# Two norms taken by token tile, the placing of crowded experts spread over four experts, and the last norm of block two read from its scatter banks

## The reference, cut to what matters

```python
def _rms(x, g):
    return x * rsqrt(mean(x * x, -1) + 1e-6) * g

x = x + mixed @ w_out                                         # stage "wo"
x = x + _mem_xattn(_rms(x, cross_norm_g), _rms(mem, ..), ..)  # norm "c", stages "mq", heads, "mo"
x = x + _hier_moe(_rms(x, ffn_norm_g), ..)                    # norm "r", routing, 32 experts
x = _rms(x, final_norm_g)
...
mod = silu(c) @ w_ada + b_ada                                 # stages "ada0" to "ada11"
...
# end of block two, alpha = 2 ** 0.25
ffn = hierarchical_moe(u2, ...)                               # 32 experts, 2 of them for a token
x = layernorm(alpha * x + g2 * ffn, ln2_g, ln2_b)
```

## Time and profile before

| what | value |
|---|---|
| median of three runs | 1096.92 us |
| the profiled execution, its time | 1097.21 us |
| its span | 1095.4 us |
| PE busy in the span | 979.4 us (89%) |
| DVE busy | 570.0 us (52%) |
| ACT busy | 362.1 us (33%) |
| POOL busy | 25.1 us (2%) |
| moved by DMA | 289.02 MB |

### The profile page before, as it was taken

How to read it: one execution, slowest core, us unless ns; L and a number is a source line. 1 busy time by engine, 2 the same in 40 slices (tenths; PEclk the granted TensorE clock), 3 DMA queues, 4 the chain that set the end, 5 groups by cost and what they waited for, 6 DMA issues and landing times. The chain is left out here.

```text
span 1095.4 us, 14594 instructions
## 1 busy us (share of the span) xinstructions
PE 979.4 (89%) x5138; PEld 588.3 (54%) x5138; DVE 570.0 (52%) x1067; ACT 362.1 (33%) x682; POOL 25.1 (2%) x49
## 2 busy tenths in 40 slices
PE   6999998988988799989999899988489998999962
PEld 5677558878665433433443588756444343344432
DVE  5844446554345444455444665866654445444436
ACT  5654244443332222211222457633332221122210
POOL 1000000000000000000000000000000000000001
PEclk9999999998995899999999999969589999999987
DMA  9264671444625599999999457311419999999800
GB/s 361 92 286 156 230 269 71 161 169 158 230 115 190 214 388 428 424 422 428 425 424 384 154 183 314 150 84 68 202 60 383 429 425 424 424 427 424 337 1 39
DMA packets 28607, 289.02 MB, mean 264 GB/s; under 512 B 3049, under 2 KB 5513, under 8 KB 7441
## 3 DMA queue, kind: packets, MB, share of 16 engines
q1 hardware_dynamic: 24768, 280.99, 62.9%
q0 software_dynamic: 1424, 4.79, 1.4%
q10 hardware_dynamic: 2368, 2.64, 0.7%
HBM read 287.34 MB, written 1.06 MB: 263 GB/s over the span
## 5 line engine op out<-in xcount | busy, mean ns | idle before, releaser
L942 PE MATMUL bank<-ring,arena 128*64 128x512 f32 x1040 | 242.5, 609 | 10.4 <-DVE arena L2114 6.6
L2128 DVE TENSOR_REDUCE arena<-bank 128x512 f32 x130 | 83.8, 686 | 142.1 <-PE bank L962 140.1
L477 DVE TENSOR_TENSOR ring_r<-ring,ring_r 128x1024 fp32r<-128x1024 f32 (+1 forms) x84 | 99.2, 1211 | 91.2 <-ACT ring_r L470 91.2
L942 PEld LDWEIGHTS bank<-ring,arena 128*64 128x64 f32 x1040 | 70.6, 139 | 136.9 <-issue 136.9
L956 PE MATMUL bank<-ring,arena 128*64 128x512 f32 x520 | 128.6, 616 | 8.3 <-DVE arena L2143 6.9
L606 PE MATMUL bank<-HT_r,ring_r 128*128 128x256 f32 x352 | 103.7, 295 | 10.3 <-DVE arena_r L1744 3.8
L470 ACT ACTIVATE ring_r<-ring 128x1024 fp32r<-128x1024 f32 (+1 forms) x84 | 84.9, 1047 | 83.4 <-PE bank L608 83.2
L608 PE MATMUL bank<-HT_r,ring_r 128*128 128x256 f32 x352 | 101.8, 289 | 0.0
L1499 ACT ACTIVATE arena<-bank 128x512 f32<-128x512 f32 x64 | 38.2, 597 | 167.9 <-PE bank L942 167.9
L1505 ACT ACTIVATE arena<-bank 128x512 f32<-128x512 f32 x64 | 38.2, 597 | 147.9 <-PE bank L956 147.9
L962 PEld LDWEIGHTS bank<-tab,arena 128*128 128x128 f32 x520 | 55.8, 140 | 53.7 <-issue 51.1
(11 more groups left out here) (403 smaller groups left out, 1350.4 us busy)
## 6 DMA issues: line engine op xcount, KB each, us to landing
ring<-in_experts SPq DMA_DIRECT2D x64, 2048.0 KB, 12.8
ring<-in_experts SPq DMA_DIRECT2D x64, 1024.0 KB, 9.2
ring<-in_ada SPq DMA_DIRECT2D x12, 2048.0 KB, 7.4
ring<-in_win SPq DMA_DIRECT2D x5, 2048.0 KB, 9.6
ring<-in_hy SPq DMA_DIRECT2D x3, 2048.0 KB, 18.8
ring<-in_mk SPq DMA_DIRECT2D x2, 2048.0 KB, 8.5
ring<-in_mv SPq DMA_DIRECT2D x2, 2048.0 KB, 10.0
ring<-in_wo SPq DMA_DIRECT2D x2, 2048.0 KB, 7.4
```

The lines of the kernel that those rows point to most:

```text
L477: nc.vector.tensor_tensor(R(w), w, R(h), ALU.subtract).then_inc(sem("w_low"), 1)
L942: last = mm(gu_bank[g:g + WIN, :], xw[:, k, :], w[:, k * 512:(k + 1) * 512], start=k < 2, stop=k >= KD - 2)
L2128: last = V.reduce_sum(ysT[:, 4 * u:4 * u + 4, bass.ds(s, WIN)], dT_bank[u][:, :].rearrange("p (c g w) -> p c w g", c=4, g=2), AXX)
```

## The change

1. `token_out` takes, in the last chunk alone, tile 0 with both `k` first and then tile 1.
2. Norms "c" and "r": ACT takes squares of half tiles (512 columns), the first halves between two `high` chunks, the second halves as soon as they are added; ACT computes the root of tile 0 and of tile 1 apart, and DVE inverts it (`deviations`, `scaled`). POOL has no part in it. For "c", DVE does `low(mq0, (0, 1))` before the last two additions and not behind them. ACT loads the table for roots before, and the table for exponentials behind.
3. `ada(6)` moves to between the `wo` product and the transposes, `ada(7)` to between the `mo` product and the transposes; their column sums go behind the transposes of "c" and behind the router product. `ada6` moves ahead of `mq0` in the ring, `ada7` behind `mo1`.
4. `extra_windows` is split into four parts that stand in experts 4 to 7 of the unrolled start of the loop, which DVE now has for eight experts and not for four.
5. DVE copies the columns of the first placed window before its last two `y_window`s, in both blocks, whether there is such a window or not. For this it waits for the table and reads `n` earlier; so does PE.
6. Block two: PE puts `alpha * X` into the scatter banks. DVE empties both down banks and multiplies with `g2row` while doing so; ACT's half is gone. DVE waits for `g2r` before the experts.
7. The end of block two: tile 0 gets its moments on DVE from the banks, tile 1 on ACT from the banks (copies with sums, then squares with sums). Each tile gets its own root on ACT, DVE scales in halves of 512 columns, and SP issues four stores of 256 KB.

```diff
-    + [(n, 4096) for n in ("mk0", "mk1", "mv0", "mv1", "wo0", "wo1", "mq0", "mq1", "ada6", "ada7", "mo0", "mo1",
+    + [(n, 4096) for n in ("mk0", "mk1", "mv0", "mv1", "wo0", "wo1", "ada6", "mq0", "mq1", "mo0", "mo1", "ada7",
                            "ada8", "ada9")]
...
+            for t in range(TT):
+                for u in range(2):
+                    sp.wait_ge(sem("x_end"), 2 * t + u + 1)
+                    sp.dma_start(out[t * P:(t + 1) * P, u * 512:(u + 1) * 512], X[:, t, u * 512:(u + 1) * 512]
+                                 ).then_inc(sem("stored"), 16)
...
-                        for a in range(2):
+                        last_chunk = c == CHUNKS - 1
+                        for t, a in sorted(itertools.product(range(TT), range(2)), key=lambda ta: ta if last_chunk else ta[::-1]):
                             k = 2 * c + a
-                            for t in range(TT):
...
+            ada(6)
             transposed("cT", XN, KD, "xn_c")
+            ada_col(6)
             channel_out("mq", ["mq0", "mq1"], HT, low_m, banks_of("cT"))
...
             token_out("mo", ["mo0", "mo1"], oT, low_m, [(f"xv{h}", 0) for h in range(XH)])
+            ada(7)
...
+                mm(acc[j][:, :], ident if b == 1 else alpha, X[:, j // 2, (j % 2) * 512:(j % 2 + 1) * 512],
+                   start=True, stop=False)
...
+            def half_squares(stage, u, t, sums):
+                ready(act, stage, 2 * u + t)
+                cols = slice(u * 512, (u + 1) * 512)
+                square(XN[:, t, cols], X[:, t, cols], sums[:, 2 * u + t:2 * u + t + 1])
+            def deviations(stage, sums, eps, dev, n):
+                for t in range(TT):
+                    half_squares(stage, 1, t, sums)
+                    act.wait_ge(sem("eps"), n)
+                    act.wait_ge(sem("squares"), squared[0])
+                    A_(dev[:, t:t + 1], sums[:, 2 + t:3 + t], ACT.Sqrt, scale=1.0 / D, bias=eps[:, t:t + 1]
+                       ).then_inc(sem("dev"), 1)
             high(act, "wo0", (2, 3))
-            high(act, "wo1", (0, 1, 2, 3))
+            high(act, "wo1", (0, 1, 2))
+            for t in range(TT):
+                half_squares("wo", 0, t, ssq_c)
+            high(act, "wo1", (3,))
+            act.wait_ge(sem("zeros"), 1)
+            link(A_(idle, eps_2, ACT.Sqrt))
             high(act, "mq0", (0, 1))
-            squares("c", lambda t: X[:, t, :], lambda t: XN[:, t, :], ssq_c,
-                    lambda t: (ready(act, "wo", t), ready(act, "wo", 2 + t)))
+            deviations("wo", ssq_c, eps_c, dev_c, 1)
+            ada_evac(6)
...
+            def scaled(tag, dev, rstd, done):
+                for t in range(TT):
+                    dve.wait_ge(sem("dev"), DEVS.index((tag, t)) + 1)
+                    link(V.reciprocal(rstd[:, t:t + 1], dev[:, t:t + 1]))
+                    V.tensor_scalar(XN[:, t, :], X[:, t, :], rstd[:, t:t + 1], None, ALU.mult).then_inc(sem("normed"), 1)
...
                 def evac_down(e, first=False):
                     dve.wait_ge(sem(f"down_done{b}"), e + 1)
                     if not first:
                         dve.wait_ge(sem(f"yT_done{b}"), e)
-                    V.tensor_copy(d_sb[:, 512:1024], d_bank[1][:, :]).then_inc(sem(f"d_hi{b}"), 1)
+                    if b == 2:
+                        V.tensor_tensor(d_sb[:, 0:512], d_bank[0][:, :], g2row[:, 0:512], ALU.mult).then_inc(sem(f"d_lo{b}"), 1)
+                    evac_high().then_inc(sem(f"d_hi{b}"), 1)
...
+                experts(2 * RING, NE)
                 hidden(NE - 1)
+                dve.wait_ge(sem("routed"), b)
+                n = dve.value_load(tabi[0:1, 48:49], min_val=0, max_val=NX - 1)
+                dve.wait_ge(sem(f"gu_done{b}"), NE - 1)
+                dve.wait_ge(sem(f"xwin{b}"), NE + 1)
+                extra_x(0)
                 y_window(NE - 2)
                 evac_down(NE - 1)
                 y_window(NE - 1)
...
+            def last_norm(t, mean, sub):
+                for u in range(2):
+                    ps = got(dve, "sct2", 2 * t + u)
+                    cols = slice(u * 512, (u + 1) * 512)
+                    link(V.scalar_tensor_tensor(out=X[:, t, cols], in0=ps[:, :], scalar=mean,
+                                                in1=ROW[:, cols], op0=sub, op1=ALU.mult))
+                root(3, t)
+                for u in range(2):
+                    cols = slice(u * 512, (u + 1) * 512)
+                    V.scalar_tensor_tensor(out=X[:, t, cols], in0=X[:, t, cols], scalar=rstd_n[3][:, t:t + 1],
+                                           in1=ROW[:, 1024 + u * 512:1536 + u * 512], op0=ALU.mult, op1=ALU.add
+                                           ).then_inc(sem("x_end"), 1)
```

228 lines of the change are left out of this document (122 added, 106 removed).

## The result

The changed kernel took 1061.76 us (median of 4 runs, 1060.50 to 1063.67) against 1095.80 us (4 runs, 1093.68 to 1097.15): a ratio of 0.969, 95% interval 0.9668 to 0.9712. The forecast was 1066.7 us, with a range of 1058.5 to 1077.0 (the forecast's own, narrower range was 1063 to 1071). The profiled execution took 1063.01 us, its span 1061.0, which is 34.4 us less than the span before.

A forecast was written before the change was run, and what follows sets the result against it. PE was taken as the bound, 89% busy with about 116 us idle, and its clock. Gains 4.4 + 3.4 + 4.5 + 9.9 - 0.4 + 2.1 + 6.4 = 30.3 gave 1066.7 us, range 1058.5 to 1077.0.

The forecast's parts named there:

- rival 1: Clock stays full through block one's routing, so C gains 9.4 rather than 4.5: 1062 us; chance 0.2.
- G: End of block two: shorter moments, root and scaling before the last store, gain 6.4 us, bounds 4.4 to 8.4.
- A: Norm "c": shorter chain, ada(6) in the idle stretch, transposes and first query chunk at full clock; gain 4.4 us.
- B: Memory heads: ada(6) and ada(7) leave them, not all comes back; gain 3.4 us, between 2.0 and 3.6.
- C: Norm "r" and routing: chain 3.0 us shorter, perhaps a warmer clock; gain 4.5 us, range 0.9 to 9.4.
- D: Both expert loops: extra_windows in parts hides in DVE's idle time; gain 9.9 us, range 8 to 10.
- Rival 3: Expert loops: removing the stall exposes weight loads, D gives half back in each block, 1072 to 1076 us; chance 0.08.
- E: End of block one, start of block two's loop: early copy, loads and waits lose 0.4 us, bounds 0 and 1.
- F: Block two's placed window: earlier gate and up at full clock; gain 2.1 us, bounds 4.5 and a loss of 1.

The follow-up runs named there:

- e1: The kernel before with one edit alone, extra_windows split into four parts in experts 4 to 7: 1083.72 us against 1097.21, ratio 0.9875.
- e4: The changed kernel with ada(6) and ada(7), their column sums and ring places back in the first two memory heads: 1065.63 us.
- e7: The changed kernel with its four stores of 256 KB issued by POOL instead of SP: 1064.07 us.
- e2: The changed kernel with the placing (extra_windows) back in one piece between experts 15 and 16: 1075.63 us.
- e10: The changed kernel with four useless reductions of a down bank on DVE before every evacuation of block two's loop: 1091.30 us.
- e9: The changed kernel with two useless reductions of a down bank on DVE before every evacuation of block two's loop: 1066.31 us.
- e6: The changed kernel with two stores of 512 KB by SP instead of four of 256 KB: 1064.52 us.
- e11: The changed kernel with ada(8) moved from behind block one's router product to ahead of it: 1060.44 us.
- e8: The changed kernel with the copy for the first placed window behind the last evacuation instead of ahead of the last two y_windows: 1064.05 us.
- e12: The changed kernel with the edits of e8 and e11 together: 1058.32 us, ratio to the kernel before 0.9651.

## Why the prediction was right, and where a size was off

The measured time lies in the range for 8 in 10 and 1.2 us outside the forecast's own range of 1063 to 1071. It is the 1062 of rival 1, but rival 1 is not what happened: its clock did not come, and the time was made up elsewhere, mostly in G. That the sum came within 5 us owes something to chance, since misses of both signs are in it.

**A, 4.4 forecast, 4.3 found.** 2.3 from `wo`'s end to the query product, and 2.0 behind it, since the same heads took 53.9 us with the first chunk at half clock and 51.9 in e1, where the clock had recovered. The chain and its idle of 1.6 were right. The reason for the clock is not shown: I gave it to `ada(6)` in the gap, with which the transposes took 2.00 us in all eleven profiles, but e4 shows it full behind a bare gap of 3.46. The gap of 4.75 halved it in both profiles of the old norm (3.65 and 3.24 us for the transposes).

**B, 3.4 forecast, 4.5 found**, above my upper bound of 3.6. A head with `ada` takes 7.2 us and one without 4.1, so 6.2 us went (I had counted 5.9), and only 1.70 came back, as a new wait in front of head 0's transpose. I had expected a second such wait in head 1. Before and after:

```profile
283.10 1.92 PE L729 MATMUL bank<-ring,cm 128*32 128x512 f32 x16
...
290.30 1.92 PE L729 MATMUL bank<-ring,cm 128*32 128x512 f32 x16
...
297.53 0.66 PE L801 MATMUL bank<-tab,arena 128*128 128x128 f32 x4
```

```profile
282.91 0.66 PE L808 MATMUL bank<-tab,arena 128*128 128x128 f32 x4 [1.70 <-DVE arena L2048]
...
287.00 0.66 PE L808 MATMUL bank<-tab,arena 128*128 128x128 f32 x4
...
291.09 0.66 PE L808 MATMUL bank<-tab,arena 128*128 128x128 f32 x4
```

**C, 4.5 forecast, 2.9 found.** The chain's 3.0 came out to 0.1 us. The 1.5 that I added for a warmer clock did not come in this pair of profiles; the time of the router-to-ranks stretch varies with the clock from 16.4 to 21.5 for the code before and 18.7 to 22.8 for the changed one, and was 17.5 in e4. Rival 1 (clock full throughout) came in no profile of the changed kernel. The Trainium skill ("TensorE: Matmul & The Clock Gate", section "HAM oscillation — how this bites in real kernels") explains a falling clock by gaps without matmuls. In this trace that does not suffice: it fell within 32 matmuls of 36 columns behind no gap above 1.05 us. And the earlier trace rows, from which I read that a gap of 3.00 leaves the clock full, held for that execution and e7 alone. The `mo` product behind this gap takes 22.2 or 22.3 us in these two, and 23.7 to 24.9 in the other twelve; in the changed profile its first matmul takes 0.76, and the window behind it has the clock at half:

```profile
302.00:304.00 2.00, 2.00 (x6) 1.62 (x5) 0.00 (x0) 0.00 (x0) 0.00 (x0) 0.50 0.00 0
```

**D, 9.9 forecast, 9.9 in the pair of profiles** (4.87 + 5.07 in the spacings), 8.9 alone (e1), 10.5 when undone (e2). Hidden where I had said, and in plain experts with room, 2.16 us (e10). In the experts with a part I had counted with 1.2 to spare, and e9 shows 1.1 in three of them together. Rival 3 was real but small: 0.55 us in e1, none in the changed kernel's two profiles, and 0.1 to 0.2 us in e6, e10 and e11 (a last spacing of 7.26, 7.16 and 7.15). Its 24.6 us of slack was mis-sized: the loads have 21.0.

**E, 0.4 forecast, 0.3 found** in block one (4.87 less 4.6), and by e8 it is the early copy.

**F, 2.1 forecast, 3.1 found.** All idle before the placed product went (16.35 to 14.74, 1.6), and 1.4 behind it, where the half clock was. The 1.4 doesn't always come: in e6 and e11, with the same code there, a down product ran at half clock and the stretch took 16.9 and 17.1 us, like the 16.9 before, and not 15.5. e8 shows that the early copy gives away 0.9 of it.

**G, 6.4 forecast, 10.0 found** (with 0.1 in the scatter), outside my bounds of 4.4 to 8.4. This is the step that was mis-sized, and in one sentence: "What follows the last store is as before." Behind DVE's last row 5.39 us became 2.45, of which 2.1 come from the engine that issues (e7), and 0.6 from the size (e6).

DVE's stretch shrank by 6.9 us, near the 6.4, but by two errors that cancel. I had the banks full 1.5 us later, which doesn't show: DVE reads the first bank 1.2 us before PE's end in the kernel before and 1.3 after. And the chain behind the first bank takes 8.27 us where my sum left it 7.2. DVE is through with tile 0 at 1055.2, ACT with tile 1 at 1055.3, so neither of the two has time to spare.

My sentence that the trace does not agree in size was a wrong reading. The Trainium skill's "DMA: Bandwidth & Descriptors", section "Anatomy of one DMA", gives for POOL's path a fixed 2.0 us and the bytes at 436 GB/s, which by estimate is 2.6 us for 256 KB and 3.2 for 512. That is the landing, and I had set against it the 5.1 us from the issue to the end of the span. The landing of 512 KB on POOL before took the 3.2,

```profile
out<-X POOLq DMA_DIRECT2D x2, 512.0 KB, 3.2
```

and 256 KB took 2.4 (e7). On SP the sizes differ by the same 0.6, 2.6 against 2.0. What the sum lacked is the time behind the landing, 1.9 us with POOL and 0.4 with SP.

Sum: 4.3 + 4.5 + 2.9 + 9.9 - 0.3 + 3.1 + 10.0 = 34.4. Stretches of the same code lost 2.3 + 1.5 + 0.4 and won 2.7 + 1.6 (the last is block two's first gate and up product at full clock): together nothing. So the forecast's 30.3 was 4 us short, 3.6 of it in G; B and F were 2.1 above and C 1.6 below.

## What to carry to other kernels

Work that stands in one piece on an engine with spare time in every iteration costs the part of its length that the spare time doesn't hide, and the clock behind it (here 3.3 us of 6.3 us, and about 1.7 for a product at half clock); in pieces no longer than that spare time it costs nothing, and how much can be spared is found by adding useless work until the spacing grows. When the last instruction of a program is a store, the engine that issues it is part of the sum. And compare the same code in several profiles before a clock is explained: here stretches that nobody touched moved by up to 5 us.

## What was not expected of the hardware

The end of the span comes some 1.9 us after the landing of a last store issued by POOL (1.6 or more in the kernel before), and 0.4 after one issued by SP; the landing itself takes 2.4 and 3.2 us for 256 and 512 KB on POOL, 2.0 and 2.6 on SP. The clock stayed at its upper level behind an idle stretch of 3.46 us (e4), fell in 12 of 14 profiles behind one of 3.00 us, and fell inside a run of 32 small matmuls. It stayed at its upper level for all of that run when 16 matmuls of 512 columns went just ahead (e11, e12), and once without them (e4).
